# The opening of a two-block model on one Trainium2 core: sums over partitions with the data as TensorE's standing operand and one moving column

## The reference, cut to what matters

```python
cos, sin = rope_tables(positions)            # angle = position * inv_freq
c_act = silu(c)
mod = einsum('bd,de->be', c_act, w_ada) + b_ada            # 6 * 1024 values
sh1, sc1, g1, sh2, sc2, g2 = split(mod, 6)
h = rms_norm(x, g_pre_mix) * (1.0 + sc1) + sh1             # x is 1024 tokens x 1024 features
proj = einsum('bsd,de->bse', h, w_in)                      # the next stage
```

## Time and profile before

| | before |
|---|---|
| device time, median of 3 runs | 3034.39 us (3029.42 to 3040.65) |
| device time of the profiled execution | 3021.66 us |
| its span, first to last instruction | 3019.9 us |
| TensorE busy with matmuls | 2831.3 us, 94% |
| VectorE busy | 1938.8 us, 64% |
| ScalarE busy | 1307.0 us, 43% |
| mean granted TensorE clock | 0.977 |

### The profile page before, as it was taken

How to read it: one execution, slowest core, us unless ns; L and a number is a source line. 1 busy time by engine, 2 the same in 40 slices (tenths; PEclk the granted TensorE clock), 3 DMA queues, 4 the chain that set the end, 5 groups by cost and what they waited for, 6 DMA issues and landing times. The chain is left out here.

```text
span 3019.9 us, 45306 instructions
## 1 busy us (share of the span) xinstructions
PE 2831.3 (94%) x18392; PEld 2252.8 (75%) x18392; DVE 1938.8 (64%) x2907; ACT 1307.0 (43%) x1908; POOL 235.5 (8%) x427
## 2 busy tenths in 40 slices
PE   7999858898999999989999999998899999999998
PEld 4776734577788788867778788887677888878886
DVE  7768888656776466784777524655646567655676
ACT  3026955457655434453441113222323565543344
POOL 0003620001100000000000001110000010000000
PEclk9999879999999999999999999998999999999999
DMA  7520100235666788731453331114224556667884
GB/s 251 173 84 29 36 1 1 84 112 174 216 224 233 280 259 298 254 120 53 136 161 125 122 110 52 57 48 117 105 91 146 187 196 226 234 247 262 287 296 155
DMA packets 195950, 471.31 MB, mean 156 GB/s; under 512 B 31584, under 2 KB 60384, under 8 KB 189408
## 3 DMA queue, kind: packets, MB, share of 16 engines
q1 hardware_dynamic: 178848, 392.94, 39.4%
q0 software_dynamic: 16896, 75.51, 6.2%
HBM read 344.09 MB, written 124.29 MB: 155 GB/s over the span
## 5 line engine op out<-in xcount | busy, mean ns | idle before, releaser
L2079 PE MATMUL psum<-merged_operand 128*128 128x512 f32 x1536 | 362.5, 391 | 5.8 <-ACT h_half L2332 5.8
L2079 PEld LDWEIGHTS psum<-merged_operand 128*128 128x128 f32 x1536 | 289.4, 188 | 67.6 <-issue 6.6
L2079 PE MATMUL psum<-h_half_operand 128*128 128x512 f32 x1344 | 316.8, 391 | 0.0
L2079 PEld LDWEIGHTS psum<-h_half_operand 128*128 128x128 f32 x1344 | 252.3, 188 | 55.5 <-issue 1.0
L2079 PE MATMUL psum<-h_half_operand,weight_parts_operand 128*128 128x512 f32 x768 | 180.0, 395 | 8.1 <-DVE weight_parts_operand L2564 4.1
L2079 PEld LDWEIGHTS psum<-h_half_operand,weight_parts_operand 128*128 128x128 f32 x768 | 144.5, 189 | 42.7 <-DVE weight_parts_operand L2564 7.3
L235 DVE CAST weight_high<-weight_ring 128x1024 fp32r<-128x1024 f32 (+1 forms) x64 | 37.9, 592 | 196.6 <-PE psum L3508 105.3
L3508 PE MATMUL psum<-h_high,weight_high 128*128 128x512 f32 x480 | 151.8, 397 | 1.4 <-DVE h_low L248 1.4
L3508 PE MATMUL psum<-h_low,weight_high 128*128 128x512 f32 x480 | 148.0, 390 | 0.0
L3508 PE MATMUL psum<-h_high,weight_low 128*128 128x512 f32 x480 | 147.9, 389 | 0.0
L2564 DVE TENSOR_TENSOR weight_parts_operand<-weight_ring,weight_parts_operand 128x1024 fp32r<-128x1024 f32 x66 | 80.7, 1223 | 94.4 <-ACT weight_parts_operand L2228 94.0
(11 more groups left out here) (614 smaller groups left out, 6218.4 us busy)
## 6 DMA issues: line engine op xcount, KB each, us to landing
o<-in_w_ff SPq DMA_DIRECT2D x80, 512.0 KB, 4.5
merged<-hidden_terms SPq DMA_DIRECT2D x56, 512.0 KB, 5.8
hidden_upper<-in_w_ff_down SPq DMA_DIRECT2D x48, 512.0 KB, 4.5
weight_ring<-in_w_out SPq DMA_DIRECT2D x32, 512.0 KB, 3.6
hidden_terms<-weight_parts POOLq DMA_DIRECT2D x16, 1024.0 KB, 7.7
hidden_terms<-weight_ring POOLq DMA_DIRECT2D x16, 1024.0 KB, 7.6
hidden_upper<-in_w_ff_up SPq DMA_DIRECT2D x32, 512.0 KB, 4.6
o<-hidden_terms SPq DMA_DIRECT2D x28, 512.0 KB, 6.0
```

The lines of the kernel that those rows point to most:

```text
L2079: mm = pe.matmul(bank, w[:, at:at + P], tiles(r, i), start=opens and m == 0, stop=closes and m == 2, skip_group_check=resumed)
```

## The change

The block `load_setup` is gone: its two transfers and its semaphore increments stand at the head of `opening`, and each engine waits for `setup` itself. The squares now stand in TensorE and one column of ones moves, so the sums come out with tokens on partitions, one column for each of 8 token tiles. `Ln` and `Exp` work on 128x8, and 8 matmuls with the identity moving spread the roots over all partitions into PSUM, from which VectorE scales x. VectorE adds 6 slabs instead of 8. The slabs 6 to 15 stand in TensorE, 8 matmuls each with one column of `silu_c` moving, and add up in PSUM as columns, with `part` summed into the same bank. The row, its copy and its turning are gone. The cosine is made on ScalarE as the sine of a quarter turn less the absolute angle. `stay_busy` has 20 matmuls instead of 16.

```diff
-def load_setup(nc, K):
-    with nc.Block() as block:
-            sp.dma_start(K.cols[:], K.dram["cols"]).then_inc(K.setup.sem, 16)
-            sp.dma_start(K.consts[:], K.dram["consts"]).then_inc(K.setup.sem, 16)
-            sp.wait_ge(K.setup.sem, 32)
...
+    ADDED = KT - 2
...
             def _(sp):
+                sp.dma_start(K.cols[:], K.dram["cols"]).then_inc(K.setup.sem, 16)
+                sp.dma_start(K.consts[:], K.dram["consts"]).then_inc(K.setup.sem, 16)
                 sp.dma_start(pos_i[:], K.dram["positions"].broadcast_to([P, S])).then_inc(K.load_done.sem, 16)
...
             def _(pe):
+                def add_slab(s, bank, first, last):
+                    pe.wait_ge(K.slab_loaded[s % RING].sem, loaded0[s % RING] + 16 * (s // RING + 1))
+                    k = s % KT
+                    for t in range(KT):
+                        mm = pe.matmul(psum[:, bank, t:t + 1], K.ring[:, s % RING, t * P:(t + 1) * P],
+                                       silu_c[:, k:k + 1], start=first and t == 0, stop=last, skip_group_check=True)
+                    mm.then_inc(K.slab_used.sem, 1)
+                pe.sem_inc(K.slab_used.sem, RING)
+                pe.wait_ge(K.setup.sem, 32)
                 for t in range(KT):
                     pe.wait_ge(K.sq_ready.sem, sq0 + t + 1)
-                    for h in range(2):
-                        mm = pe.matmul(psum[:, 4 + h, :], K.const("ones"), sq[:, t % 2, h * HALF:(h + 1) * HALF],
-                                       start=(t == 0), stop=(t == KT - 1))
+                    for b in range(NT):
+                        mm = pe.matmul(psum[:, 1, b:b + 1], sq[:, t % 2, b * P:(b + 1) * P], K.const("ones")[:, 0:1],
+                                       start=(t == 0 and b == 0), stop=(t == KT - 1), skip_group_check=True)
                     mm.then_inc(K.sq_used.sem, 1)
+                pe.wait_ge(K.root_ready.sem, root0 + 2)
+                for b in range(NT):
+                    mm = pe.matmul(both(4)[:, b * P:(b + 1) * P], root[:, b:b + 1].broadcast_to([P, P]),
+                                   K.const("ident"), start=True, stop=True)
+                mm.then_inc(K.pe_done.sem, 1)
                 pe.wait_ge(K.act_done.sem, act0 + 1)
-                pe.wait_ge(K.slab_used.sem, used0 + RING + KT)
-                for k in range(KT):
-                    s = KT + k
-                    pe.wait_ge(K.slab_loaded[s % RING].sem, loaded0[s % RING] + 16 * (s // RING + 1))
-                    for h in range(2):
-                        mm = pe.matmul(psum[0:1, 2 + h, :], silu_c[:, k:k + 1],
-                                       K.ring[:, s % RING, h * HALF:(h + 1) * HALF], start=(k == 0), stop=(k == KT - 1))
...
+                pe.wait_ge(K.slab_used.sem, used0 + RING + ADDED)
                 for t in range(KT):
-                    mm = pe.matmul(psum[:, 7, t:t + 1], row[:, t * P:(t + 1) * P], K.const("ones")[0:1, 0:1],
-                                   start=True, stop=True)
-                mm.then_inc(K.pe_done.sem, 1)
-                K.stay_busy(pe, 0, 16)
+                    pe.matmul(psum[:, 6, t:t + 1], part[:, t * P:(t + 1) * P], K.const("ones")[:, 0:1],
+                              start=(t == 0), stop=False, skip_group_check=True)
+                for s in range(ADDED, KT):
+                    add_slab(s, 6, False, s == KT - 1)
+                for s in range(KT, LATER):
+                    add_slab(s, 7, s == KT, s == LATER - 1)
+                K.stay_busy(pe, 0, 20)
...
             def _(act):
+                act.wait_ge(K.setup.sem, 32)
                 act.activation(silu_c[:], K.col("c", 0, KT), ACT.Silu).then_inc(K.act_done.sem, 1)
+                act.activation(root[:, 0:1], K.col("eps"), ACT.Ln)
...
-                act.activation(root, psum[:, 4:6, :].rearrange("p b f -> p (b f)"), ACT.Ln, scale=1.0 / D,
-                               bias=K.col("eps")).then_inc(K.root_ready.sem, 1)
+                act.activation(root[:], psum[:, 1, 0:NT], ACT.Ln, scale=1.0 / D, bias=K.col("eps")) \
+                    .then_inc(K.root_ready.sem, 1)
...
+                act.activation(cos[:], sin[:], ACT.Abs).then_inc(K.act_done.sem, 1)
+                act.activation(cos[:], cos[:], ACT.Sin, scale=-1.0, bias=quarter[:]).then_inc(K.act_done.sem, 1)
+                act.activation(sin[:], sin[:], ACT.Sin).then_inc(K.act_done.sem, 1)
```

More of the change, by code:

```diff
@@ L208, in __call__ @@
         self.wait()
-def load_setup(nc, K):
-    with nc.Block() as block:
-        @block.sync
-        def _(sp):
-            sp.dma_start(K.cols[:], K.dram["cols"]).then_inc(K.setup.sem, 16)
-            sp.dma_start(K.consts[:], K.dram["consts"]).then_inc(K.setup.sem, 16)
-            sp.wait_ge(K.setup.sem, 32)
[L220 to L228, removed]
 def split(dve, chain, x, high, low):
@@ L589, in opening @@
         pos_i = K.sbuf(ctx, "positions_int", [P, S], I32)
-        part, row, sq = room[:, 0, :], room[0:1, 1, :], room[:, 2:4, :]
-        root, angle, turns = (room[:, n, :] for n in (4, 5, 6))
+        root = K.sbuf(ctx, "token_root", [P, NT])
+        quarter = K.sbuf(ctx, "quarter_turn", [P, 1])
+        part, sq = room[:, 0, :], room[:, 2:4, :]
+        angle, turns = (room[:, n, :] for n in (5, 6))
         landed = [K.shared_flag(f"landed_{n}") for n in range(4)]
         landed0 = [f.n for f in landed]
-        row_kept, w_val_landed = K.shared_flag("mod_row_kept"), K.shared_flag("w_val_landed")
+        w_val_landed = K.shared_flag("w_val_landed")
         used0, loaded0, load0 = K.slab_used.n, [f.n for f in K.slab_loaded], K.load_done.n
@@ L599, in opening, with both @@
         at = {}
+        def both(bank):
+            return psum[:, bank:bank + 2, :].rearrange("p b f -> p (b f)")
         with nc.Block() as block:
@@ L621, in _ @@
                     mm.then_inc(K.sq_used.sem, 1)
-                pe.wait_ge(K.act_done.sem, act0 + 1)
-                pe.wait_ge(K.slab_used.sem, used0 + RING + KT)
-                for k in range(KT):
-                    s = KT + k
-                    pe.wait_ge(K.slab_loaded[s % RING].sem, loaded0[s % RING] + 16 * (s // RING + 1))
-                    for h in range(2):
-                        mm = pe.matmul(psum[0:1, 2 + h, :], silu_c[:, k:k + 1],
-                                       K.ring[:, s % RING, h * HALF:(h + 1) * HALF], start=(k == 0), stop=(k == KT - 1))
[L630 to L633, removed]
-                                           start=True, stop=True)
-                        if t == KT - 1:
-                            mm.then_inc(K.pe_done.sem, 1)
@@ L637, in _ @@
-                pe.wait_ge(row_kept.sem, row_kept.n + 1)
-                for t in range(KT):
-                    mm = pe.matmul(psum[:, 7, t:t + 1], row[:, t * P:(t + 1) * P], K.const("ones")[0:1, 0:1],
-                                   start=True, stop=True)
-                mm.then_inc(K.pe_done.sem, 1)
-                K.stay_busy(pe, 0, 16)
+                pe.wait_ge(K.root_ready.sem, root0 + 2)
+                for b in range(NT):
+                    mm = pe.matmul(both(4)[:, b * P:(b + 1) * P], root[:, b:b + 1].broadcast_to([P, P]),
+                                   K.const("ident"), start=True, stop=True)
@@ L646, in _, with add_to_part @@
                 c = Chain(dve, K.dve_done)
[L648 to L658, removed]
+                def add_to_part(k):
                     dve.wait_ge(K.slab_loaded[k % RING].sem, loaded0[k % RING] + 16 * (k // RING + 1))
@@ L667, in _, with scale @@
                     ins.then_inc(K.slab_used.sem, 1)
-                reduce_angle(dve, c, cos[:], turns, angle, 0.25)
-                at["cos"] = c.n
+                def scale(t):
+                    dve.wait_ge(K.pe_done.sem, pe0 + 1)
+                    c.step(dve.tensor_tensor(out=x[:, t, :], in0=x[:, t, :], in1=both(4), op=ALU.mult))
+                dve.wait_ge(K.load_done.sem, load0 + 16)
+                c.step(dve.memset(quarter[:], float(np.pi / 2)))
+                c(dve.tensor_copy(angle, pos_i[:]))
+                dve.wait_ge(K.setup.sem, 32)
+                c(dve.tensor_scalar(angle, angle, K.col("inv_freq"), None, op0=ALU.mult))
+                reduce_angle(dve, c, sin[:], turns, angle, 0.0)
+                at["angle"] = c.n
+                dve.wait_ge(K.act_done.sem, act0 + 1)
+                for k in range(ADDED):
+                    add_to_part(k)
                 for t in range(KT):
                     scale(t)
-                dve.wait_ge(K.pe_done.sem, pe0 + 1)
+                dve.wait_ge(K.slab_used.sem, used0 + RING + KT)
                 c.step(dve.tensor_tensor(out=K.mod[:, 0:KT], in0=psum[:, 6, 0:KT], in1=K.col("b_ada", 0, KT), op=ALU.add))
-                dve.wait_ge(K.pe_done.sem, pe0 + 2)
+                dve.wait_ge(K.slab_used.sem, used0 + RING + LATER)
                 c(dve.tensor_tensor(out=K.mod[:, KT:2 * KT], in0=psum[:, 7, 0:KT], in1=K.col("b_ada", KT, KT), op=ALU.add))
```

(18 more changed lines are left out.)

## The result

The changed kernel takes 3061.83 us, the median of 5 runs (3057.93 to 3071.74), against 3032.36 us before (5 runs, 3028.61 to 3040.65). The ratio is 1.0099, 95% interval 1.0082 to 1.0115: slower by 1%, some 30 us. The forecast was 3067, range 3050 to 3077.

A forecast was written before the change was run, and what follows sets the result against it. TensorE bounds the kernel, with matmuls in flight for 94% of the span. The opening's terms, mostly one-column matmuls at the low clock, sum to +32.6 us on the 3034.4 us median: 3067 us, range 3050 to 3077.

The forecast's parts named there:

- first matmul of the squares: Start of the opening: positions issued 2.8 us earlier by the merged setup, first x tile at 11.4 us, first matmul at 12.5.
- squares: TensorE in the opening: 128 instructions from a cold start at 0.211 us each, 27.0 us, ending at 39.5.
- roots: After the squares: two small activations, one table load and semaphores on ScalarE, 1.85 us, with TensorE now waiting.
- spread, start to the next group's start: TensorE spreading the roots over partitions: 16 instructions of 128 columns at 0.215 us, 3.4 us, ending at 44.8.
- `part` and slabs: TensorE after the spread: 88 matmuls, 176 instructions at 0.211 us, 37.1 us, ending at 81.9.
- from there to the third block: End of the opening: `stay_busy` from a cold start until 88.5 us, then 0.7 to the third block's first matmul.
- third block, against before: Sum of the opening's terms: third block's first matmul at 89.2 us instead of 56.6, +32.6 us.
- The step that carried the forecast: TensorE's opening: one moving column neither raises nor holds the clock, so instructions cost 0.211 us instead of 0.111.
- full-speed rival: TensorE's opening: clock reaches 2.4 GHz some 4 us into the squares and stays; +0.9 us, not slower; chance 0.07.
- the lower bound's case: Spread of the roots: clock may rise there and hold about 4.0 us into the one-column run, -3.6 us.
- The covers: VectorE's slabs, scaling x, the cosine's absolute value and slab transfers cost nothing, hidden behind TensorE; VectorE or transfers 18 us early.
- What had a chance of 0.89: Whole kernel: slower by more than about 0.5% (15 us), 0.86 for the summed loss plus 0.03 from an intermittent-clock rival.

## Why the prediction was right, point by point

| term | forecast | measured |
|---|---|---|
| first matmul of the squares | 12.5 us | 13.28 |
| squares | 27.0 | 27.43 |
| roots | 1.85 | 1.88 |
| spread, start to the next group's start | 3.4 | 3.32 |
| `part` and slabs | 37.1 | 34.7 (45.91 to 80.60) |
| from there to the third block | 7.3 | 7.8 |
| third block, against before | +32.6 | +31.8 |

The step that carried the forecast was the price of 0.211 us for an instruction with one moving column at the low clock, taken from L1043; 0.214 was measured. That the clock and not the form sets it is shown from three sides: the 16 instructions of `part` have this form and took 0.115 each while the clock was up, 128 columns at the same standing operands cut the squares from 27.43 to 16.73 us, and a warm start loses the clock under one column with TensorE busy throughout. The sentence of the Trainium skill that a gapless TensorE gets 2.4 GHz ("TensorE: Matmul & The Clock Gate", section "Why this matters for your kernels") doesn't hold for this form in either trace. The 107 ns that the prediction quotes beside it stand on that page without a word on the clock; the instructions here, each with such a load, came 0.11 us apart at the full clock and 0.21 at the low one, so the figure fits the full clock alone. The full-speed rival's sum, +0.9 us, is roughly that of the form at full clock, though: with 128 copies the third block moved by +5.4 us from a cold start and by -1.4 from a warm one, at ratios of 1.0000 and 0.9985.

Three terms were off, and they cancel in part. The start was 0.8 us late: the merged setup moves x by 2.1 us, not 2.8, which is between the bounds given. `part` and the slabs were 2.4 us short, because the clock did rise as the spread of the roots ended and held over `part` and most of the first slab (41 instructions between 45 and 50 us). That was the lower bound's case, at -3.6. `stay_busy` took 7.62 us instead of 6.6, since the clock rose some 6 us into it and not 4, and the gap behind it was 0.4 us shorter than assumed. That the opening's sum came within 0.8 us is therefore partly luck. The medians moved by 29.5 us and the profiled spans by 38.6, so a device time could not tell terms of this size apart; the timeline could.

The covers held. VectorE's `part` ended at 26.6 (19.76 + 6.85) against 45.9 when TensorE read it; the scaling ended at 55.2 against 80.6; the absolute value for the cosine ran behind the roots, from 42.44 us, with nothing but the two sines behind it until 81.04.

What had a chance of 0.89, slower by over 0.5%, came: the interval's low end, 1.0082, lies above that bound. One outcome doesn't tell whether the chance was well placed.

## What to carry to other kernels

Before a matmul is turned round so that the data stands and a vector moves, look in the trace for the same form elsewhere and read the granted clock beside it. At 2.4 GHz the two forms cost about the same here (9.10 us for 5 slabs with 128 copies, 1.82 each, against 1.88 before), so the clock decides. Where the turned form is wanted, moving 128 copies of the column costs 0.115 us an instruction at the full clock instead of 0.21 at the low one; against the kernel before, that brought the time back and won next to nothing. A few microseconds won at the start of a chain count only when the next block starts. Look at what ends last ahead of the barrier: here it was `stay_busy`, whose results nobody uses; at the low clock it outlasted the real work by 2.4 us in one profile and 3.3 in another.

## What the runs showed of the hardware that was not expected

Raising the clock and keeping it are different things. In one profile 64 moving columns ran for 27.5 us from a cold start without it rising, and the same 64 columns kept it for 16 us once 128 had raised it, in two profiles. And a busy TensorE at the low clock gives itself away in the count of instructions before the clock column does, as that column shows 1.00 until the first recorded change.
